# Two transformer blocks on one core: scale of the chunk attention moved to its queries, squares behind transposes, another first microsecond, phase ends with settings of their own

## What is computed

```python
def first_block(x, ...):
    for l in range(DEPTH):                         # DEPTH = 2
        h = x @ w_in[l]
        rq, rk, rv, rg, cq, ck, cv, dq, dk, dv, gates = split(h)
        o_a = _retention(rq, rk, rv, rg, ret_norm_g[l])
        o_b = _chunk_attention(cq, ck, cv, ca_rel_bias[l])   # softmax(cq ck^T / 8 + bias)
        o_c = _diff_attention(dq, dk, dv, lam, ...)
        merged = sum of sigmoid(gate) * (o @ w_branch) over a, b, c
        x = _layer_norm(ALPHA * x + merged @ w_out[l], ln1)
        x = _layer_norm(ALPHA * x + (silu(x @ w_gate) * (x @ w_up)) @ w_ffn_out[l], ln2)
    return x

def hybrid_layer(h, p_i, ...):                     # second block, twice
    h = h + 0.5 * swiglu(rmsnorm(h, ffn1_norm), ...)
    z = rmsnorm(h, mix_norm) @ w_in
    hm, ha = mLSTM branch of z, sliding-window attention branch of z
    h = h + (sigmoid(g_m) * (hm @ w_branch_m) + sigmoid(g_a) * (ha @ w_branch_a)) @ w_out
    h = h + 0.5 * swiglu(rmsnorm(h, ffn2_norm), ...)
    return h + sigmoid(rmsnorm(h, ple_norm) @ ple_gate_w) * (p_i @ ple_proj_w)
```

## Time and profile before

| | us |
|---|---|
| median of 3 runs | 2388.64 (2388.24 to 2388.89) |
| the profiled execution | 2387.63 |
| its span, from the first to the last instruction | 2385.8 |
| PE busy | 2359.8 |
| DVE busy | 1457.3 |
| ACT busy | 1213.2 |
| POOL busy | 139.7 |

### The profile page before, as it was taken

One profiled execution on the slowest core, in us unless ns is written; L12 is line 12 of the kernel. 1 busy time (PEld: TensorE's weight loads), 2 busy tenths in 40 slices (PEclk: granted clock), 3 DMA queues, 4 the chain that ended last, 5 costly groups with the idle time before them and its releaser, 6 DMA issues.

```text
span 2385.8 us, 30340 instructions
## 1 busy us (share of the span) xinstructions
PE 2359.8 (99%) x11608; PEld 1975.4 (83%) x11608; DVE 1457.3 (61%) x2224; ACT 1213.2 (51%) x1838; POOL 139.7 (6%) x133
## 2 busy tenths in 40 slices
PE   8999999999999999999999999999999999999999
PEld 7888878878888888788888888888888889888887
DVE  5556775565557855565487656654755577556554
ACT  5555544435556444354466654544544476555443
POOL 1430000014210000000000000000000000000000
PEclk9999999999999999999999999999999999999999
DMA  8545456545455565555554445655555544445553
GB/s 299 167 152 198 163 202 234 185 160 170 159 190 168 179 221 184 169 186 193 170 191 145 159 142 168 208 184 180 203 190 190 176 160 142 159 155 190 177 194 106
DMA packets 118078, 427.55 MB, mean 179 GB/s; under 512 B 13616, under 2 KB 14384, under 8 KB 116912
## 3 DMA queue, kind: packets, MB, share of 16 engines
q1 hardware_dynamic: 117792, 425.56, 52.9%
q10 hardware_dynamic: 144, 0.07, 0.0%
HBM read 424.52 MB, written 1.05 MB: 178 GB/s over the span
## 4 chain that ended last, share of the span: by engine, by line
PE 95%; DVE 3%; ACT 1%; DMA 1%; issue 0%; POOL 0%; DVEq 0%; ACTq 0%
PE bank L1878 28%; PE bank L1880 27%; PE bank L1879 27%; PE bank L1935 5%; PE bank L1866 1%; PE bank L1867 1%; PE bank L1868 1%; DVE wl L1446 0%; PE bank L1980 0%; DMA raw<-in_weights 0%; PE bank L1953 0%; PE bank L2003 0%; ACT wh L1235 0%; DVE x L1611 0%; DVE xl L1458 0%
## 5 line engine op out<-in xcount | busy, mean ns | idle before, releaser
L1235 ACT ACTIVATE wh<-raw 128x1024 fp32r<-128x1024 f32 (+1 forms) x778 | 814.9, 1052 | 916.0 <-PE bank L1880 876.7
L1446 DVE TENSOR_TENSOR wl<-raw,wh 128x1024 fp32r<-128x1024 f32 (+1 forms) x778 | 939.3, 1222 | 462.1 <-ACT wh L1235 457.9
L1878 PE MATMUL bank<-wh,xh 128*128 128x512 f32 (+1 forms) x2176 | 867.2, 399 | 9.3 <-DVE xl L1458 6.1
L1880 PE MATMUL bank<-wh,xl 128*128 128x512 f32 (+1 forms) x2176 | 848.6, 390 | 0.0
L1879 PE MATMUL bank<-wl,xh 128*128 128x512 f32 (+1 forms) x2176 | 846.7, 389 | 0.0
L1878 PEld LDWEIGHTS bank<-wh,xh 128*128 128x128 f32 x2176 | 410.4, 189 | 91.8 <-issue 12.5
L1880 PEld LDWEIGHTS bank<-wh,xl 128*128 128x128 f32 x2176 | 410.0, 188 | 86.3
L1879 PEld LDWEIGHTS bank<-wl,xh 128*128 128x128 f32 x2176 | 411.0, 189 | 78.1
L1878 PE MATMUL bank<-wh,act_h 128*128 128x512 f32 x528 | 207.1, 392 | 0.0
L1880 PE MATMUL bank<-wh,act_l 128*128 128x512 f32 x528 | 205.6, 389 | 0.0
L1879 PE MATMUL bank<-wl,act_h 128*128 128x512 f32 x528 | 205.5, 389 | 0.0
(11 more groups left out here) (339 smaller groups left out, 2233.9 us busy)
## 6 DMA issues: line engine op xcount, KB each, us to landing
raw<-in_weights SPq DMA_DIRECT2D x760, 512.0 KB, 3.3
raw<-in_weights SPq DMA_DIRECT2D x16, 384.0 KB, 3.0
ln<-in_ln SPq DMA_DIRECT2D x4, 1024.0 KB, 6.4
bias<-in_bias SPq DMA_DIRECT2D x2, 1024.0 KB, 10.5
b_merge<-in_b_merge SPq DMA_DIRECT2D x2, 1024.0 KB, 5.6
gain<-in_gain_ffn SPq DMA_DIRECT2D x4, 512.0 KB, 3.8
decay<-in_decay SPq DMA_DIRECT2D x2, 768.0 KB, 12.0
x<-in_x SPq DMA_DIRECT2D x2, 512.0 KB, 5.1
```

The costliest lines, as they stand in the source:

```text
L1235: act.activation(wh[:, u % NH, 0:used(u)], raw[:, u % NR, 0:used(u)], ACT.Copy).then_inc(hi_done, 1)
L1446: dve.tensor_tensor(wl[:, u % NR, 0:used(u)], raw[:, u % NR, 0:used(u)], wh[:, u % NH, 0:used(u)].bitcast(F32), ALU.subtract).then_inc(lo_ ...
L1878: pe.matmul(out, h, w_h, start=st.first and i == 0, stop=False)
L1880: last = pe.matmul(out, lo, w_h, start=False, stop=st.last and i == st.nk - 1)
```

## The change

It has five parts. (1) The scale 1/8 of the chunk attention is put on the queries when ACT copies their transposes (`turn`, `scale=CDH ** -0.5`); the score step multiplies by 1.0, the mask is NEG, and POOL's multiply of `bias` is gone. (2) The two squares that followed an `rms` step for `which == 0` (end of block 1, and `ple`) are moved behind the transposes of the same tile. (3) At the beginning PE multiplies zeros: four fp32 matmuls of 128x256 first and three before the first unit, from a buffer that DVE clears; the identity is loaded by SP ahead of `x`. (4) The first unit's tile 0 runs its four `wh` matmuls first, waiting for `hi_done` alone, and then, after `lo_done`, its two `wl` matmuls. (5) Some phase ends get other numbers, and the end of block 1 and the first FFN of each second-block layer get rows of their own.

```diff
+WARM = (4, 3)
...
-TAILS = {"branch_c": (4, 2, 3, 3), "w_out_1": (8, 6, 4, 5), "ffn_1": (6, 5, 4, 4),
-         "branch_m": (8, 5, 3, 5), "w_out_2": (8, 4, 3, 3), "ffn_2": (8, 3, 4, 5),
-         "ple": (5, 2, 4, 5)}
-OPEN = {"w_in_1": 7, "ffn_1": 6, "w_in_2": 6, "ffn_2": 6}
+TAILS = {"branch_c": (4, 1, 2, 3), "w_out_1": (8, 6, 4, 5), "ffn_1": (6, 5, 4, 4),
+         "branch_m": (8, 5, 3, 5), "w_out_2": (8, 2, 3, 3), "ffn_2": (8, 3, 3, 5),
+         "ple": (5, 3, 4, 5), "change": (6, 5, 5, 5), "ffn_2a": (8, 3, 4, 6)}
+OPEN = {"w_in_1": 7, "ffn_1": 6, "w_in_2": 6, "ffn_2": 6, "change": 7}
...
         p.add("rms", which=which, tile=tile, n=fed[tile], m=gained)
-        if which == 0:
-            for j in range(2):
-                p.add("square", tile=tile, j=j, n=p.count("sumsq"), fed=None if p.suffix else fed[tile],
-                      m=p.cc["ple"] if p.suffix else None)
+        fed["ple", tile] = p.cc.get("ple")
...
         last = p.turns("merged", "x", KT, tile, fed=fed[tile])
+        if which == 0:
+            for j in range(2):
+                p.add("square", tile=tile, j=j, n=p.count("sumsq"), fed=fed[tile], m=fed["ple", tile])
...
+                sp.dma_start(ident[:, :], a["ident"]).then_inc(ident_loaded, 16)
                 sp.dma_start(x[:, 0, :], xin[:, 0, :]).then_inc(x_loaded[0], 16)
...
-                        link(pool.tensor_scalar(b["bias"][:, :, :], b["bias"][:, :, :], CDH ** 0.5, None, ALU.mult))
-                        pool.memset(b["bias"][0:CHUNK, :, 192:256], NEG * CDH ** 0.5).then_inc(bias_up, 1)
+                        pool.memset(b["bias"][0:CHUNK, :, 192:256], NEG).then_inc(bias_up, 1)
...
-                act.dma_start(ident[:, :], a["ident"]).then_inc(ident_loaded, 16)
...
+                                       TB[st.t % 2][:, :].rearrange("p (k n) -> p k n", k=4), ACT.Copy,
+                                       scale=CDH ** -0.5 if st.src == "cq" else 1.0).then_inc(t_done[st.t % 2], 1)
...
+                dve.memset(b["gt"][:, 0, 0, :], 0.0).then_inc(zeros, 1)
...
+                            scale = 1.0 if k == "ca_s" else DDH ** -0.5
...
+                pe.wait_ge(zeros, 1)
+                for _ in range(WARM[0]):
+                    pe.matmul(OB[:, 0:256], b["gt"][:, 0, 0, 0:P], b["gt"][:, 0, 0, 256:512], start=True, stop=True)
...
+                    if st.kind == "first_tile" and not st.u:
+                        for _ in range(WARM[1]):
+                            pe.matmul(OB[:, 0:256], b["gt"][:, 0, 0, 0:P], b["gt"][:, 0, 0, 256:512], start=True, stop=True)
...
+                        if not st.u and k == "first_tile":
+                            pe.wait_ge(hi_done, 1)
+                            out = DB[2 * st.pair][:, 0:st.n]
+                            for i in range(st.nk):
+                                for w in (lh, ll):
+                                    pe.matmul(out, w[:, i, 0:P], wh[:, 0, i * st.n:(i + 1) * st.n],
+                                              start=i == 0 and w is lh, stop=False)
+                            pe.wait_ge(lo_done, 1)
+                            for i in range(st.nk):
+                                last = pe.matmul(out, lh[:, i, 0:P], wl[:, 0, i * st.n:(i + 1) * st.n], start=False, stop=False)
+                            last.then_inc(first_done, 1)
+                            continue
```

More of the change, by code:

```diff
@@ L485, in plan_block1 @@
     t_x = plan_ffn(p, "w_ffn_in", "w_ffn_in", "w_ffn_out", F1, F1, t_x2, ALPHA, 1.0, after_down, chain,
-                   turned(p, 0, fed), stats=True)
+                   turned(p, 0, fed), stats=True, end="change")
     return t_x
@@ L511, in turned, with plan_ffn @@
     return add
-def plan_ffn(p, w_gate, w_up, w_down, width, up_at, t_x, old, new, after_in, chain, turned_of, scaled=None, stats=False):
+def plan_ffn(p, w_gate, w_up, w_down, width, up_at, t_x, old, new, after_in, chain, turned_of, scaled=None, stats=False,
+             end="ffn_1", opening="ffn_1"):
     nch = -(-width // 256)
@@ L536, in plan_ffn @@
             p.steps = kept
-            p.open(group, OPEN["ffn_1" if stats else "ffn_2"])
+            p.open(group, OPEN[opening])
         if c == 4:
@@ L552, in plan_ffn @@
             turn_chunk(nch - 1)
-    k = TAILS["ffn_1" if stats else "ffn_2"][0]
+    k = TAILS[end][0]
     group, p.steps = p.steps[-k:], p.steps[:-k]
@@ L564, in plan_ffn @@
     group.append(evac)
-    return p.tail(group, chain, turned_of, *TAILS["ffn_1" if stats else "ffn_2"])
+    return p.tail(group, chain, turned_of, *TAILS[end])
 def plan_block2(p, t_x):
@@ L581, in ffn @@
         return plan_ffn(p, name + "_w_gate", name + "_w_up", name + "_w_down", F2, None, t_x, 1.0, 0.5, after_in,
-                        lambda tile: rms(p, which + 1, tile, fed), turned(p, which + 1, fed), scaled=p.cc["scaled"])
+                        lambda tile: rms(p, which + 1, tile, fed), turned(p, which + 1, fed), scaled=p.cc["scaled"],
+                        end="ffn_2" if which else "ffn_2a", opening="ffn_2" if which or l else "change")
     def after_ffn1():
@@ L863, in build @@
         ident_loaded = sem("ident_loaded")
+        zeros = sem("zeros")
         rope_loaded = sem("rope_loaded")
@@ L1253, in _ @@
                         act.activation(b[st.dst][:, :, st.tile * P:st.tile * P + P],
-                                       TB[st.t % 2][:, :].rearrange("p (k n) -> p k n", k=4), ACT.Copy)\
-                           .then_inc(t_done[st.t % 2], 1)
+                                       TB[st.t % 2][:, :].rearrange("p (k n) -> p k n", k=4), ACT.Copy,
+                                       scale=CDH ** -0.5 if st.src == "cq" else 1.0).then_inc(t_done[st.t % 2], 1)
                     elif k == "ret_gate":
@@ L1509, in _ @@
                             add = b["bias"][:, n, :] if k == "ca_s" else b["dmask"][:, :]
-                            dve.tensor_tensor_reduce(b["Pn"][:, n % 4, 0:256], bank[:, 0:256], add, 0.125, -3e38,
+                            scale = 1.0 if k == "ca_s" else DDH ** -0.5
+                            dve.tensor_tensor_reduce(b["Pn"][:, n % 4, 0:256], bank[:, 0:256], add, scale, -3e38,
                                                      ALU.add, ALU.max, mx[:, 2 * (n % 8) + 1:2 * (n % 8) + 2])
                             dve.tensor_tensor_reduce(b["Pn"][:, n % 4, 256:384], bank[:, 256:384], add[:, 128:256],
-                                                     0.125, -3e38, ALU.add, ALU.max, mx[:, 2 * (n % 8):2 * (n % 8) + 1])\
+                                                     scale, -3e38, ALU.add, ALU.max, mx[:, 2 * (n % 8):2 * (n % 8) + 1])\
                                .then_inc(s_done if bank is SB else t_done[st.t % 2], 1)
@@ L1845, in _ @@
                             turned(st.after_t)
+                        lh, ll = split_of[st.lhs]
+                        if not st.u and k == "first_tile":
[10 more added lines that the diff above has]
+                            continue
                         pe.wait_ge(lo_done, st.u + 1)
@@ L1848, in _ @@
                             pe.wait_ge(p_ready, 2 * (st.l + 1))
-                        lh, ll = split_of[st.lhs]
                         sh, sl = st.u % NH, st.u % NR
```

## The result

| us | before | changed |
|---|---|---|
| median | 2388.24 (2386.96 to 2388.89, 5 runs) | 2376.06 (2375.03 to 2376.19, 5 runs) |
| the profiled execution | 2387.63 | 2376.19 |
| its span | 2385.8 | 2374.4 |
| PE busy | 2359.8 | 2358.4 |

The ratio is 0.9948, with a 95% interval of 0.9934 to 0.9963: faster by 12.2 us, more than the 0.2% that can be told from no change.

A forecast was written before the change was run, and what follows sets the result against it. PE, busy 2359.8 of 2385.8 us, bounds the kernel, so only its stops and clock count. 2.8 + 4.9 + 1.9 + 0.4 + 0.4 - 0.2 = 10.2 us off 2388.64 gives 2378.4 us, range 2376.2 to 2381.5.

The forecast's parts named there:

- Part 3: End of block 1, near 1000 us: squares behind transposes and new end numbers; 2.9 us if the clock holds, 1.9 taken.
- the 1.2 and the 0.7 us waits: Behind the xl wait near 1000 us: PE waits 1.2 us for tile 1's merged, then 0.7 for wl.
- rival (a): Near 1007 us: the clock holds behind the 2.5 us wait, total 2377.4 us; chance 0.27.
- Part 4: Other phase ends: ffn_2 gains 0.4 us, ple 0.4, ffn_2a -0.2, w_out_2 and branch_c 0.
- The two waits of 0.23 us and the one of 0.43: PE's xl waits at ffn_2 in two layers and merged wait at ple go: gains 0.4 and 0.4 us.
- `ffn_2a`: At this end, tile 1's chain may start 0.1 us later, twice: -0.2 us.
- `w_out_2` and `branch_c`: Transposes sooner at these ends; w_out_2's merged 1.0 us ahead, branch_c between 0 and -0.3 us; both taken as 0.
- Part 1: Beginning: zeros, earlier first real matmul on wh and high clock; loads perhaps 0.2 us later; gain 2.8 us.
- Part 2: Near 510 us: without POOL's multiply, PE waits 0.9 instead of 4.17 us and half clock goes; gain 4.9 us.
- Rival (c): At 511.04 us: POOL is not what held DVE, wait and slow clock stay, total 2383.3 us; chance 0.05.

The follow-up runs named there:

- the larger memset: Changed kernel plus a POOL memset of all of bias, 128x2048, where the multiply stood; 2376.46 us.
- ffn_1_5: Changed kernel with the end of layer 0's FFN (near 500 us) on behind 5 and ahead 5 instead of 4 and 4; 2374.81 us.
- combined: Changed kernel with behind 5 instead of 4 at both w_out_1 ends, FFN opening with seven units instead of six, identity on ACT's queue; 2374.50 us.
- both ends changed: Changed kernel with w_out_1 at 8,6,5,5, ffn_1 at 6,5,5,5, and its FFNs opening with seven units; 2374.79 us, changed kernel beside it 2376.05.

## Why the prediction was right and wrong

Direction, order of size and the places were right: the three large terms stood where they were put, and no wait of a new kind appeared. The time was missed, by terms that were mis-sized.

**Part 3, the price of the clock (1.9 predicted, 2.88 seen).** The wait (2.5 predicted, 2.55) and the three `wl` were as worked out, and the clock did fall. The step that failed is "some 5 us of work at half clock add 2.5, of which the 1.2 and the 0.7 us waits swallow most": the low stretch was 3.4 us, PE worked in 3.2 of it, which loses 1.6, and the waits to come took all of it: with the clock up and with the clock down PE comes out within 0.04 us. Forecast and rival (a) were in truth one case at this place; 1.0 us of the range's low side was spent on a difference that isn't there. The 5 us are the length of the stretch behind 515.20, where PE had stood 4.17 us.

**Part 4, brackets taken for prices (0.6 predicted, 1.7 seen).** The two waits of 0.23 us and the one of 0.43 were entered as 0.4 and 0.4. They cost 0.48, 0.46 and 0.78. That matmuls overlap stood in the reading of the profile, and the sum did not use it for the 0.43 at all, and too little for the two of 0.23. The prediction also gave `ple`'s gain to the number alone and 0 to the squares, where the runs show that each needs the other. `ffn_2a` was put at -0.2 and was 0 between the first traces, within what the loader does there; `w_out_2` and `branch_c` at 0 held, with the slack of 1.0 us as read.

**Part 1 (2.8 predicted, 2.35 seen; 1.1 to 2.6 with the other executions).** Zeros, early `wh` and full pace came as said. `x` and the first units landed 0.5 us later than before, not 0.2, in this trace (`x` at 5.10 instead of 4.61). And the old pass over tile 0 was over at 22.80, not 22.94: the row at 22.80 is already the first matmul of tile 1, so 0.14 us of the gain was a misreading. Most of the uncertainty isn't in the change: the kernel before itself finishes its beginning 0.76 us apart in two executions.

**Part 2 (4.9 predicted, 4.8 against the same trace, 4.0 to 5.1 by others).** Right in cause and in its rows (the wait for `wl` was 0.50, not 0.7). That the size came so near is in part luck: it took the low stretch as long as that one trace had it. Rival (c) fell.

**The sum and the range.** The terms' errors add to +1.0, +1.1, -0.45 and, with the loader's waits, -0.4: 11.5 us by the two traces. The other 0.7 us to the measured 12.2 are that the profiled execution of the kernel before took 0.6 us less than the median of its five runs, and that of the changed kernel 0.1 more; the later comparisons gave 10.8 and 12.5. Between this 12.2 and the 2.3 us by which the forecast was missed there is 0.4 more: the forecast started from 2388.64, the median of three runs, and that of five is 2388.24. The prediction carried 1.0 us for such a difference into the time, but the range had no term for it. With 0.5 us either way for where an execution stands, its low end would have been below the result.

## What to carry to other kernels

Price a short wait by the starts of the instructions on both sides of it, not by its bracket; where instructions overlap the bracket can be half the cost. Before charging for a slow stretch, ask what its engine would meet at full pace: if another engine is busy without a hole there, slow work only replaces waiting, as at 1000 us; where nothing is due, as at 513 us, it costs half of what PE works in it. And give two executions of the same kernel a term of their own in the range, when the sum is a half per cent of the time.

## What the runs showed of the hardware

- The granted clock fell in some executions and not in others behind the same wait: near 1000 us, behind 2.55 us, it fell in the changed kernel's three traces and in six others, and stayed in four that have the same rows there (the larger memset, the identity on ACT's queue, ffn_1_5 and combined); behind 1.88 us it fell with both ends changed and stayed in ffn_1_5. The Trainium skill, "TensorE: Matmul & The Clock Gate", section "Why this matters for your kernels", which the prediction weighed, asks for a longer gap than either; these traces don't agree with it.
- The clock can fall after PE is back at work: with the multiply back PE stood 2.55 us and started at 1005.70, and the clock was at 1.00 until 1006.7 and at 0.50 from 1006.8 to 1010.1.
- A POOL operation that reads and writes 128x2048 fp32 held DVE's two-input operations for 3.2 us (4.67 instead of 1.42 for the two); one that only writes it, 1.81 us long, held them not at all.
- The first weight unit landed at 6.25, 6.39 and 6.93 us in the changed kernel's three traces. In its later places the loader varies too, and with it PE's waits near 314 (0.39, 0, 0.24 us), 503 (1.34, 1.13, 1.41) and 809 us (0.69, 0.46, 0.76).
